# Four last column tiles of an input projection in another order, with the value transposes moved ahead of the last of them

## The reference

```python
def hybrid_layer(x, ...):
    x = x + 0.5 * swiglu(rmsnorm(x, ffn1_norm), ffn1_w_gate, ffn1_w_up, ffn1_w_down)
    z = rmsnorm(x, mix_norm) @ w_in                       # 2048 columns
    q, k, v, p_in, c_in, d_in = jnp.split(z, [G, 2 * G, 3 * G, 4 * G, 6 * G], axis=-1)   # G = 256
    q = rmsnorm(q.reshape(B, T, ATT_HEADS, HEAD_DIM), q_norm)
    k = rmsnorm(k.reshape(B, T, ATT_HEADS, HEAD_DIM), k_norm)
    att = moba_attention(q, [k_past, k], [v_past, v], pos0)       # softmax with ALiBi; past blocks from a paged cache
    pool, pool_state = pool_mixer(pool_hist, p_in, pool_w, pool_scale)     # window means 2/4/8/16, minus the token
    conv, conv_state = conv_module(conv_hist, c_in, ...)          # GLU, depthwise 31, LayerNorm, swish, pointwise
    gmlp, gate_v = spatial_gating(d_in, gate_norm, spatial_w, spatial_b)
    x = x + jnp.concatenate([att, pool, conv, gmlp], axis=-1) @ w_out
    x = x + 0.5 * swiglu(rmsnorm(x, ffn2_norm), ffn2_w_gate, ffn2_w_up, ffn2_w_down)

def spatial_gating(d_in, gate_gain, spatial_w, spatial_b):
    u, v = jnp.split(jax.nn.gelu(d_in), 2, axis=-1)
    v = rmsnorm(v, gate_gain)
    s = (causal spatial_w @ v within chunks of 128) + spatial_b
    return u * s, v
```

## Time and profile before

| | us |
|---|---|
| median of 3 timed runs | 1197.0 (1196.15 to 1201.56) |
| profiled execution, its own time | 1203.46 |
| its span, first to last instruction | 1201.6 |
| PE busy | 1171.2 (97%) |
| POOL busy | 808.6 (67%) |
| DVE busy | 634.1 (53%) |
| ACT busy | 530.7 (44%) |
| PE's wait for DVE's take of z_v (L611) | 3.3, two times |
| PE's wait for the input split on DVE (L538) | 18.6, eight times |

### The profile page before, as it was taken

How to read it: one execution, slowest core, us unless ns; L and a number is a source line. 1 busy time by engine, 2 the same in 40 slices (tenths; PEclk the granted TensorE clock), 3 DMA queues, 4 the chain that set the end, 5 groups by cost and what they waited for, 6 DMA issues and landing times.

```text
span 1201.6 us, 23236 instructions
## 1 busy us (share of the span) xinstructions
PE 1171.2 (97%) x7924; PEld 1143.8 (95%) x7924; DVE 634.1 (53%) x897; ACT 530.7 (44%) x778; POOL 808.6 (67%) x424
## 2 busy tenths in 40 slices
PE   5999999999999999999999999999998999999999
PEld 4999999999889999999999999999986999999998
DVE  6657773137976544432255777612679664445100
ACT  4544444443655344444444444444446554444332
POOL 4876767766856766667677676677577466666674
PEclk9999999999999999999999999999999999999999
DMA  7544435457235544435555444455672354444453
GB/s 255 163 149 148 152 114 146 151 187 210 85 108 176 158 146 151 144 118 151 158 180 164 149 141 147 122 154 167 187 220 70 110 156 148 151 148 134 134 147 111
DMA packets 70970, 180.57 MB, mean 150 GB/s; under 512 B 9866, under 2 KB 24850, under 8 KB 70930
## 3 DMA queue, kind: packets, MB, share of 16 engines
q1 hardware_dynamic: 70640, 178.97, 47.5%
q10 hardware_dynamic: 290, 1.10, 0.2%
HBM read 176.45 MB, written 3.58 MB: 150 GB/s over the span
## 4 chain that ended last, share of the span: by engine, by line
PE 90%; DVE 8%; DMA 1%; issue 1%; ACT 1%; SPq 0%; DVEq 0%; ACTq 0%
PE bank L538 29%; PE bank L541 29%; PE bank L539 29%; DVE xg_lo L1011 2%; DVE bank L1088 1%; DVE sumsq L1019 1%; DMA x<-in_xT 1%; DVE prob L1222 0%; PE bank L742 0%; PE bank L695 0%; PE bank L586 0%; DVE qk L1182 0%; DVE prob L1196 0%; DVE tmp L1231 0%; PE bank L718 0%
## 5 line engine op out<-in xcount | busy, mean ns | idle before, releaser
L434 POOL TENSOR_TENSOR w_lo<-raw,w_hi 128x1024 fp32r<-128x1024 f32 (+2 forms) x352 | 766.6, 2182 | 374.8 <-ACT w_hi L813 374.8
L813 ACT ACTIVATE w_hi<-raw 128x1024 fp32r<-128x1024 f32 (+2 forms) x352 | 338.4, 962 | 481.3 <-PE bank L541 453.8
L538 PE MATMUL bank<-xg_hi,w_hi 128*128 128x320 f32 x1664 | 521.4, 313 | 18.6 <-DVE xg_lo L1011 18.6
L539 PE MATMUL bank<-xg_lo,w_hi 128*128 128x320 f32 x1664 | 517.2, 311 | 0.0
L541 PE MATMUL bank<-xg_hi,w_lo 128*128 128x320 f32 x1664 | 517.1, 311 | 0.0
L538 PEld LDWEIGHTS bank<-xg_hi,w_hi 128*128 128x128 f32 x1664 | 314.4, 189 | 24.3 <-issue 12.7
L539 PEld LDWEIGHTS bank<-xg_lo,w_hi 128*128 128x128 f32 x1664 | 314.5, 189 | 0.8
L541 PEld LDWEIGHTS bank<-xg_hi,w_lo 128*128 128x128 f32 x1664 | 314.5, 189 | 0.0
L538 PE MATMUL bank<-h_hi,w_hi 128*128 128x320 f32 x704 | 217.9, 309 | 0.0
L539 PE MATMUL bank<-h_lo,w_hi 128*128 128x320 f32 x704 | 217.9, 309 | 0.0
L541 PE MATMUL bank<-h_hi,w_lo 128*128 128x320 f32 x704 | 217.8, 309 | 0.0
(11 more groups left out here) (171 smaller groups left out, 717.9 us busy)
## 6 DMA issues: line engine op xcount, KB each, us to landing
raw<-in_w SPq DMA_DIRECT2D x224, 512.0 KB, 3.8
raw<-in_w SPq DMA_DIRECT2D x64, 384.0 KB, 3.1
raw<-in_w SPq DMA_DIRECT2D x64, 320.0 KB, 2.9
k_all<-in_cache_kT SPq DMA_DIRECT2D x32, 128.0 KB, 2.8
v_past<-in_cache_v SPq DMA_DIRECT2D x32, 128.0 KB, 2.8
x<-in_xT SPq DMA_DIRECT2D x2, 640.0 KB, 6.0
cst<-in_consts ACTq DMA_DIRECT2D x1, 997.0 KB
out_yT<-x SPq DMA_DIRECT2D x1, 960.0 KB, 5.0
```

Of the source, the lines that this page charges most:

```text
L434: pool.tensor_tensor(w_lo[:, j, 0:count * P], raw[:, j, 0:count * P], w_hi[:, j, 0:count * P].bitcast(F32), ALU.subtract).then_inc(split.s ...
L538: pe.matmul(out, hi, in_hi[:, k, :], start=first and n == 0, stop=False)
L539: pe.matmul(out, hi, in_lo[:, k, :], start=False, stop=False)
L813: act.activation(w_hi[:, j, 0:count * P], raw[:, j, 0:count * P], ACT.Copy).then_inc(split_hi.sem, 1)
```

## The change

The four last tiles come in the order v, v, u, u. SP's `load_slot` can be told which of the two halves of a weight row to read; with this the loop over the last two iterations is written out in Python, so SP gets straight code. The prompt part of `value_rows` (four transposes) moves ahead of the last column and uses bank 1, waiting for 14 taken tiles; the batch part becomes `batch_value_rows`, uses bank 3, and stands behind `gate_value_rows`. On ACT the GELU of u0 leaves its place ahead of the exponentials and runs just before that of u1. Numbers in the kernel after are shifted against those before by 1 to 10 lines.

```diff
+VALUES_FIRST = ((0, 8), (8, 8), (0, 8), (8, 8))
@@ SP
-            def load_slot(L, base, i, j, weights, row, halves):
+            def load_slot(L, base, i, j, weights, row, halves, which=None):
 
                 sp.wait_ge(split.sem, L * split.per + (base + i) * 4 + j + 1)
                 first, count = halves[j]
-                src = weights[bass.ds(row, 1), j % 2, :, first * P:(first + count) * P].rearrange("a p n -> (a p) n")
+                src = weights[bass.ds(row, 1), j % 2 if which is None else which, :, first * P:(first + count) * P].rearrange("a p n -> (a p) n")
...
-                with sp.Fori(0, DEC_B // 4) as n:
+                for n in range(DEC_B // 4):
                     for j in range(4):
-                        load_slot(L, BASE_I, 2 + n, j, w8, L * W8_ROWS + (W8_I + 2) + n, HALVES8)
+                        row = L * W8_ROWS + (W8_I + 2) + n
+                        if n == 0:
+                            load_slot(L, BASE_I, 2, j, w8, row, HALVES8)
+                        else:
+                            load_slot(L, BASE_I, 3, j, w8, row, VALUES_FIRST, 1 - j // 2)
                         load_past(L, n * 4 + j)
@@ PE
             def value_rows(L):
 
+                pe.wait_ge(taken.sem, taken.at(L, T_I + 14))
+                for c in range(GT):
+                    for t in range(2):
+                        mm = pe.transpose(bank[1][:, t * 2 * P + c * P:t * 2 * P + (c + 1) * P], z_v[:, c, t * P:(t + 1) * P], ident)
+                mm.then_inc(v_tr.sem, 1)
+
+            def batch_value_rows(L):
+
                 pe.wait_ge(taken.sem, taken.at(L, T_O))
-                for c in range(GT):
-                    for t in range(2):
-                        mm = pe.transpose(bank[3][:, t * 2 * P + c * P:t * 2 * P + (c + 1) * P], z_v[:, c, t * P:(t + 1) * P], ident)
-                mm.then_inc(v_tr.sem, 1)
                 pe.wait_ge(sp_ok.sem, sp_ok.at(L, 3))
-                pe.matmul(bank[1][0:NS, 256:288]...
+                pe.matmul(bank[3][0:NS, 256:288]...
                 for c in range(GT):
-                    mm = pe.transpose(bank[1][0:NS, c * P:(c + 1) * P], z_v[:, c, SEQ:TOK], ident)
+                    mm = pe.transpose(bank[3][0:NS, c * P:(c + 1) * P], z_v[:, c, SEQ:TOK], ident)
                 mm.then_inc(v_tr.sem, 1)
...
                 conv_mean(L)
+                value_rows(L)
                 column(L, BASE_I, T_I, 1, 3, 3)
                 prompt_attention_transposes(L)
-                value_rows(L)
                 conv_variance(L)
                 gate_value_rows(L)
+                batch_value_rows(L)
                 prompt_attention(L)
@@ ACT
                 round_slot(L, BASE_O, 0, 0, HALVES8)
-                gelu(z_u[:, 0, :], T_I + 12)
...
-                act.activation(v_tok[...], bank[3][:, :], ACT.Copy).then_inc(v_copied.sem, 1)
+                act.activation(v_tok[...], bank[1][:, :], ACT.Copy).then_inc(v_copied.sem, 1)
...
-                act.activation(v_tok_s[:, :], bank[1][0:NS, 0:GT * P], ACT.Copy).then_inc(v_copied.sem, 1)
+                act.activation(v_tok_s[:, :], bank[3][0:NS, 0:GT * P], ACT.Copy).then_inc(v_copied.sem, 1)
...
-                gelu(z_u[:, 1, :], T_I + 14)
+                for c in range(GT):
+                    gelu(z_u[:, c, :], T_I + 14 + c)
@@ DVE (w_sps reads bank 3 in place of bank 1)
-                take(L, 12, z_u[:, 0, :])
+                take(L, 12, z_v[:, 0, :])
...
-                take(L, 13, z_v[:, 0, :])
+                take(L, 13, z_v[:, 1, :])
...
-                take(L, 14, z_u[:, 1, :])
+                take(L, 14, z_u[:, 0, :])
...
-                take(L, 15, z_v[:, 1, :])
+                take(L, 15, z_u[:, 1, :])
```

More of the change, by code:

```diff
@@ L606, in value_rows @@
             def value_rows(L):
-                pe.wait_ge(taken.sem, taken.at(L, T_O))
+                pe.wait_ge(taken.sem, taken.at(L, T_I + 14))
                 for c in range(GT):
                     for t in range(2):
-                        mm = pe.transpose(bank[3][:, t * 2 * P + c * P:t * 2 * P + (c + 1) * P], z_v[:, c, t * P:(t + 1) * P], ident)
+                        mm = pe.transpose(bank[1][:, t * 2 * P + c * P:t * 2 * P + (c + 1) * P], z_v[:, c, t * P:(t + 1) * P], ident)
                 mm.then_inc(v_tr.sem, 1)
+            def batch_value_rows(L):
+                pe.wait_ge(taken.sem, taken.at(L, T_O))
                 pe.wait_ge(sp_ok.sem, sp_ok.at(L, 3))
-                pe.matmul(bank[1][0:NS, 256:288].rearrange("p (g t) -> p g t", g=HEADS), views["e8"][0:8, :],
+                pe.matmul(bank[3][0:NS, 256:288].rearrange("p (g t) -> p g t", g=HEADS), views["e8"][0:8, :],
                           w_sp[0:8, :, 0:DEC_T], start=True, stop=True).then_inc(sp_rep.sem, 1)
                 for c in range(GT):
-                    mm = pe.transpose(bank[1][0:NS, c * P:(c + 1) * P], z_v[:, c, SEQ:TOK], ident)
+                    mm = pe.transpose(bank[3][0:NS, c * P:(c + 1) * P], z_v[:, c, SEQ:TOK], ident)
                 mm.then_inc(v_tr.sem, 1)
@@ L943, in _ @@
                 act.wait_ge(v_tr.sem, v_tr.at(L, 1))
-                act.activation(v_tok[:, :, :].rearrange("p t n -> p (t n)"), bank[3][:, :], ACT.Copy).then_inc(v_copied.sem, 1)
+                act.activation(v_tok[:, :, :].rearrange("p t n -> p (t n)"), bank[1][:, :], ACT.Copy).then_inc(v_copied.sem, 1)
                 act.wait_ge(v_tr.sem, v_tr.at(L, 2))
-                act.activation(v_tok_s[:, :], bank[1][0:NS, 0:GT * P], ACT.Copy).then_inc(v_copied.sem, 1)
+                act.activation(v_tok_s[:, :], bank[3][0:NS, 0:GT * P], ACT.Copy).then_inc(v_copied.sem, 1)
                 act.wait_ge(cv_var.sem, cv_var.at(L, 1))
@@ L1252, in _ @@
                 dve.tensor_tensor(w_sps[:, :, :, :],
-                                  bank[1][0:NS, 256:288].rearrange("p (g b t) -> p g b t", g=HEADS, b=1).to_broadcast([NS, HEADS, DEC_B, DEC_T]),
+                                  bank[3][0:NS, 256:288].rearrange("p (g b t) -> p g b t", g=HEADS, b=1).to_broadcast([NS, HEADS, DEC_B, DEC_T]),
                                   views["bmask"][0:NS, :].rearrange("p (g b t) -> p g b t", g=1, b=DEC_B).to_broadcast([NS, HEADS, DEC_B, DEC_T]),
```

## The result

The changed kernel takes 1207.9 us (median of 18 runs, 1204.3 to 1220.3); the kernel before, run beside it, 1197.05 (18 runs, 1196.0 to 1201.6). The ratio is 1.0109, with an interval of 1.0087 to 1.0132: 1.1% slower, 10.9 us. The forecast was 1200.5 with a range of 1193.5 to 1204, so the time lies outside it. The profiled execution of the changed kernel is not far from its timed runs: 1206.37, with a span of 1204.6. Ten of the 18 lie between 1204.3 and 1208.2; the other eight take 1211 to 1220, and seven of these have the lowest granted clocks of the 18 (means over the run of 0.982 to 0.989). On the scale of profiled executions the working had asked for 1207.

The account below looks back on a forecast made before the run. It took DVE, up to the end of prob_new, as the bound, with PE only filling in. Terms 2.8 + 0.9 - 0.1 = +3.6, rounded to +3.5, put on the median 1197.0, gave 1200.5 us, range 1193.5 to 1204.

Parts of the forecast that it names:

- I take the difference from the profile and put it on the median: Whole kernel: sums made against the profiled execution, 1203.46 us, with the difference then applied to the timed median, 1197.0.
- The last rounding: ACT's rounding of the stage's last weight slot: 2.85 us earlier in the first layer, 2.4 in the second.
- The run starts: POOL's four splits in a row: start about 2.5 us earlier in the first layer, 2.0 in the second.
- The order moves put at nothing: Tile order, banks and paired GELUs: cost 0; earlier value transposes on PE: gain 0.1 us, first layer only.
- prob_new ends: DVE, first layer: prob_new ends at 333.9 in place of 331.04, +2.8 us.
- The sum on the profile's scale: Whole kernel: 2.8 + 0.9 - 0.1 = +3.6, rounded to +3.5, giving 1207 us against the profiled execution.
- The z_w pair: DVE's two z_w products (L1236): stand behind POOL's splits, 5 us or more in place of 1.42.
- +0.9: DVE, second layer: prob_new ends at 923.7 in place of 922.82.
- the copies' gain: DVE's small copies beside POOL's last split: gain between 0 and 1.9 us, taken as 0.75 a layer.
- the six instructions: SP, six address instructions fewer per weight load: 0.13 us each, 0.8 in all; last load up to 5.5 earlier.
- No net change: Rival: DVE's z_w goes ahead of POOL's four splits, or SP gains nothing; 1197.0 us, chance 0.28.
- Slower, 1203.5: Rival: at POOL's four splits, all four DVE products stand behind splits; +6.5 us, chance 0.14.

Follow-up runs that it names:

- the kernel that excludes the stall: Kernel before with POOL's last split of slot 3 held until DVE's small copies have ended: 1196.64 us, ratio 0.9989.
- third profiled execution: Kernel before, unchanged, profiled once more: span 1203.6 us, first layer free of the stall and the second with it.
- the two experiments on it: Changed kernel with SP's loop kept: 1196.97 us; kernel before with only SP's loop written out: 1219.29 us.
- the two holds: Changed kernel with POOL's four splits held until prob_new is made: 1198.62 us; with only the last split held behind DVE's small copies: 1197.04 us.
- the copy was made to wait: Kernel before with DVE's last small copy made to wait until POOL's last split of slot 3 has ended: 1212.11 us, ratio 1.0110.

## Why the prediction was wrong

**The step that failed** is the one in its own words "I take the difference from the profile and put it on the median". The profiled execution lay 6.5 us above the median; the prediction saw this and passed over it. Those 6.5 us were a stall of the very kind that the change was being priced for: a DVE instruction behind a POOL split in each layer, and prob_new (in the second layer prob_s too) behind the run of splits as a consequence. The executions that make the median mostly have neither, by the kernel that excludes the stall and has the same median. So the change was compared with a before that already had most of the loss in it.

| | stage, layer 1 | stage, layer 2 | span |
|---|---|---|---|
| before, profiled | 32.79 | 34.67 | 1201.6 |
| before, split held behind the copies | 29.99 | 29.93 | 1193.7 |
| after | 35.63 | 34.64 | 1204.6 |

Against the undisturbed execution the change costs 35.63 - 29.99 = 5.6 and 34.64 - 29.93 = 4.7 us in the stages. With about 0.2 behind the first (46.65 in place of 46.41) that makes 10.6 of the 10.9 between the spans, and the medians differ by 10.9 as well. That the last two agree so closely is in part luck, since the median of after lies 1.5 above its profiled execution and that of the undisturbed kernel 1.1. The median of before rests on many runs: of its 114 timed executions 82 lie under 1200 us, and 16 over 1204, where its third profiled execution (1205.36) lies too.

**Right, step by step.** The loop written out is the cause, and the only one: the two experiments on it and the two holds show it from both sides. The last rounding starts 2.3 us earlier in the first layer (2.85 forecast); it still waits 2.92 for the DMA there, where PE's leaving the slot was to be the bound, as it is in the second layer. The run starts 2.75 earlier (2.5 forecast). The order moves put at nothing are at nothing (ratio 1.0004). prob_new ends at 333.30 in the first layer (333.9 forecast). The first stage grew by 2.8, as forecast, but partly by luck: prob_new came only 2.3 later, and the slow value products brought PE to L717 0.6 behind it. The sum on the profile's scale, 1207, was 0.6 from 1206.37.

**Mis-sized terms.** The z_w pair met one split and not two: 3.24 us in place of "5 us or more". Three splits were waited out, as forecast, but at the second z_w, prob_s and prob_new, since the run began 0.3 behind the first z_w and not 0.2 ahead of it. In the second layer +0.9 was forecast from the profile and the stage there did not change (34.67, 34.64), since before had two of the three stalls there already. For the same reason the copies' gain was a gain on the profile alone: in the first layer all six take 3.38 us in the profile of before and 2.71 now, 0.7 less (0.75 forecast), but 1.19 in the undisturbed execution. There they meet nothing, and now the end of the split and POOL's taps (1.54 and 0.68 for two, where 0.41 is undisturbed), so this term has the other sign on the median, some 1.5 us. SP's weight loads are 4.4 apart where nothing holds them (275.80, 280.18 and 284.60 in its queue), not 4.1 as forecast, and were 4.86; so the six instructions cost 0.08 us each and not 0.13.

**A term left out.** Nothing was said of PE's clock. In the profiled execution of the changed kernel the lower clock cost at most 0.6 us in the first stage and 0.2 behind it. In its neighbours it decided up to 13 us, and eight of its own 18 timed executions take 1211 to 1220 at mostly lower mean clocks (no trace of one was taken), so that leaving it out did little to the median was luck.

**The rivals.** "No net change" rested on DVE going ahead of the run; it is what happens with either hold. "Slower, 1203.5" named the right place but priced it from the same profile. No case was worked out from an execution without the stall, though the 6.5 us asked for one: with the undisturbed durations (0.2, 0.8 and 0.3, as the later runs show them) put in for the stalled ones, give 2.2 for the copy and 2.0 for prob_new in the first layer, and 2.4, 1.9 and 2.0 in the second, 10.5 us at most. The runs show 7.9 of it; below that PE's own work is the bound.

By the rule of the Trainium skill that the prediction named (SBUF — State Buffer, "Who interferes with whom"), whichever of the two engines issues first holds the port. The traces agree: 2.3 to 2.7 us for DVE instructions of 0.2 to 0.8 that meet a split.

## What to carry to other kernels

When the profiled execution is longer than the timed median by more than the effect at stake, find out first what is in the profile that the median does not have; a stall next to the change, decided by a tenth of a microsecond between two engines, is the first suspect. Code that gets faster on an engine with slack can start a helper's long instructions ahead of a critical engine's short ones; here one wait that keeps them behind cost nothing and took the chance out. A filler for an idle engine pays only where the idle does not just move on to the next wait.

## What the runs showed of the hardware

One small copy that meets a split (2.4 us) cost its stage 2.8 us where the delay brought one of DVE's later products into the run of splits (32.79 against 29.99), and 4.7, twice itself, where it brought two (34.73 against 30.04). In the third execution of before the split at 889.16 was issued 0.1 us behind the first of two copies at 889.07 and held up the second; in the first layer it came 0.55 behind the last copy and held up nothing. Which of the two happens is decided by the arrival of one weight load: the rounding that the split waits for was released by its DMA in both layers, 3.6 us behind the start of the stage in the first and 2.5 in the second. It changes between executions of the same kernel.

PE's granted clock fell to the lower level in idle times of 1.4 to 3.0 us or up to 4 us behind them, and stayed there for some 3 to 17 us, though PE was busy without a gap in most of it. It did not do so after each such idle: behind the 1.43 in the second layer of before it stayed at 1.00, in the third execution of the same kernel, behind 1.43 as well, it fell; and where the copy was made to wait, the same 1.43 brought a fall in the first layer and none in the second. In the changed kernel with the hold on the run it fell from 333 to 343 us with no idle over 0.91 us in that stage. Ten of the 17 traces, that of before among them (302 to 305 us), also show some 3 us of lower clock about the copies of queries and keys, with PE busy without a gap for 12 us and more ahead of it. What decides this the runs here do not settle.
